# Gate tiles first in the input projection, with the start of the recurrence between its later tiles

## What is computed

```python
h = modulate(rmsnorm(x, ln1_w), shift, scale)
p = h @ w_in                 # 18 tiles of 128 columns
# au, av : 2+2 tiles, gating MLP          bq, bkv, kr : 2+1+1, latent attention
# cq, cf, cb, ci, cg : 2 each, recurrence (query, forget gates of both directions, value, output gate)
a = au * (w_s . rmsnorm(av) + b_s)
f, k = gates(cf, cb)         # log of the forget gate; key = 1 - gate
o = scan_forward(cq, k, ci, log f) + scan_backward(...)    # in chunks of 128 tokens
b = attention(...)
x += gate * (concat(a, b, rmsnorm(o) * silu(cg)) @ w_out)
x += gate * peer(modulate(rmsnorm(x), ...))                # expert retrieval; the longest part
```

## Time and profile before

| | us |
|---|---|
| median of 3 runs (lowest, highest) | 4656.94 (4653.06, 4658.84) |
| profiled execution, its own time | 4664.94 |
| its span, first to last instruction | 4662.7 |
| PE, DVE, ACT, POOL busy | 4049.6, 3641.3, 1752.6, 1137.1 |

### The profile page before, as it was taken

How to read it: one execution, slowest core, us unless ns; L and a number is a source line. 1 busy time by engine, 2 the same in 40 slices (tenths; PEclk the granted TensorE clock), 3 DMA queues, 4 the chain that set the end, 5 groups by cost and what they waited for, 6 DMA issues and landing times. The chain is left out here.

```text
span 4662.7 us, 66977 instructions
## 1 busy us (share of the span) xinstructions
PE 4049.6 (87%) x22357; PEld 3490.8 (75%) x22357; DVE 3641.3 (78%) x7170; ACT 1752.6 (38%) x3120; POOL 1137.1 (24%) x1190
## 2 busy tenths in 40 slices
PE   7967877899789999999999976788864899999998
PEld 6865435799678888888888855633653799999998
DVE  4177665699979999999999943734599799999998
ACT  3223542210334444444444432254312444444443
POOL 0000000000964343434434400000005632333332
PEclk9956999895999999999999978599987999999999
DMA  4110112124579999999999920000212799999997
GB/s 171 50 37 27 50 54 87 40 69 136 164 260 373 376 377 368 366 371 383 373 374 376 369 67 32 18 0 0 76 52 72 272 372 373 371 371 371 375 374 282
DMA packets 246327, 1017.96 MB, mean 218 GB/s; under 512 B 16976, under 2 KB 115376, under 8 KB 145984
## 3 DMA queue, kind: packets, MB, share of 16 engines
q0 software_dynamic: 85824, 602.70, 33.4%
q1 hardware_dynamic: 160320, 413.17, 24.5%
HBM read 963.31 MB, written 52.43 MB: 218 GB/s over the span
## 5 line engine op out<-in xcount | busy, mean ns | idle before, releaser
L479 PE MATMUL psA<-h_hi,split_hi 128*128 128x448 f32 (+3 forms) x2816 | 991.7, 352 | 128.0 <-DVE xT L2247 54.9
L1206 POOL DMA_INDIRECT rows<-rows,pick_i x512 | 795.8, 1554 | 1160.6 <-DVE y_tok L2268 651.3
L1704 DVE TENSOR_TENSOR split_lo<-raw,split_hi 128x1024 fp32r<-128x1024 f32 x596 | 727.1, 1220 | 417.0 <-ACT split_hi L1247 415.4
L479 PE MATMUL psA<-h_lo,split_hi 128*128 128x448 f32 (+3 forms) x2816 | 969.6, 344 | 0.0
L479 PE MATMUL psA<-h_hi,split_lo 128*128 128x448 f32 (+3 forms) x2816 | 969.2, 344 | 0.0
L1247 ACT ACTIVATE split_hi<-raw 128x1024 fp32r<-128x1024 f32 x596 | 628.1, 1054 | 317.4 <-DMA raw<-expert_pairs 147.2
L479 PEld LDWEIGHTS psA<-h_hi,split_hi 128*128 128x128 f32 x2816 | 535.7, 190 | 216.7 <-issue 140.9
L2256 DVE CUSTOM_DVE_ANT_1 rows<-rows,h_wide 128x1024 f32<-128x1024 f32 x512 | 624.0, 1219 | 16.5 <-DMA rows<-rows,pick_i 14.2
L2268 DVE SCALAR_TENSOR_TENSOR y_tok<-rows,pick_w,y_tok 128x1024 f32<-128x1024 f32 x444 | 568.6, 1281 | 5.9
L479 PEld LDWEIGHTS psA<-h_hi,split_lo 128*128 128x128 f32 x2816 | 536.1, 190 | 38.0
L479 PEld LDWEIGHTS psA<-h_lo,split_hi 128*128 128x128 f32 x2816 | 537.2, 191 | 34.3
(11 more groups left out here) (301 smaller groups left out, 6470.4 us busy)
## 6 DMA issues: line engine op xcount, KB each, us to landing
raw<-expert_pairs SPq DMA_DIRECT2D x256, 1024.0 KB, 7.2
gates<-g_buf SPq DMA_DIRECT2D x24, 2048.0 KB, 8.7
raw<-tiles SPq DMA_DIRECT2D x84, 512.0 KB, 3.5
raw<-mod_tiles SPq DMA_DIRECT2D x80, 512.0 KB, 3.4
g_in<-gates POOLq DMA_DIRECT2D x32, 896.0 KB, 8.8
g_in<-gates POOLq DMA_DIRECT2D x32, 640.0 KB, 5.8
mod_w<-mod_pairs SPq DMA_DIRECT2D x8, 1024.0 KB, 17.8
rows<-rows,pick_i POOLq DMA_INDIRECT x512, 8.5
```

What stands on the lines that cost most here:

```text
L479: ins = nc.tensor.matmul(out_, lhsT, rhs, start=start, stop=stop)
L1206: nc.gpsimd.indirect_dma_start(rows[l][:, b, :], None, (rows0, rows1)[l], bass.IndirectOffsetOnAxis(pick_i[:, u:u + 1], 0))\
L1704: V.tensor_tensor(split_lo[:, n % SPLIT].rearrange("p k n -> p (k n)"), raw[:, n % RAW, :], split_hi[:, n % SPLIT].rearrange("p k n -> p ( ...
```

## The change

The columns of `w_in` are put in the order cf, cb, av, cq, ci, kr, bkv, bq, cg, au. Steps of the chain whose inputs are then ready are moved between the later tiles: at step 3 the clip and the logarithm, at 4 the sums, at 5 the squares' sum, the root and the exponential, at 6 the norm of av, at 7 the multiplication by the key. Splits go one tile further ahead (`split_to(IN0 + p + 4)`). Results of tiles 14 to 17 (cg in `psV`, au in `psA`) stay in PSUM until the last tile is done, since their places in SBUF lie where the projection's input is. After them PE first transposes, then does the gating product. The first two `log_decays` stand before it on DVE. `MOD_FRONT` is gone: its 8 tiles are now worked off in `route`. POOL's clearing of `states` waits for the end of the projection in place of the end of the gating part.

```diff
-MOD_FRONT, MOD_OWN = 8, 32
+MOD_OWN = 32
-MOD_AFTER = (20, 7, 7, 6)
+MOD_AFTER = (26, 8, 8, 6)
+HELD_AT = 14
-    in_cols = np.concatenate([a_u, b_q, b_kv, kr_tile, c_q, c_f, c_b, c_g, a_v, c_i])
+    in_cols = np.concatenate([c_f, c_b, a_v, c_q, c_i, kr_tile, b_kv, b_q, c_g, a_u])
...
# PE
+                elif HELD_AT <= p < HELD_AT + 2:
+                    held[l].append(seen.bank(psum_V_free))
+                    feature_tile("V", own)
...
-                for i in range(MOD_FRONT):
-                    mod_tile(psA[:, f + 1, 2 * i:2 * i + 2], (OUT0[l] + i) % RAW)
             pe.wait_ge(khat_ready, seen.upto(khat_ready))
...
+            gated_mlp(l)
             pe.wait_ge(khT_ready, seen.upto(khT_ready))
...
# POOL
-            pool.wait_ge(a_done, seen.upto(a_done))
+            pool.wait_ge(proj_ready, seen.upto(proj_ready))
             pool.memset(states[:], 0.0).then_inc(states_zero, 1)
...
# ACT
+            for p in range(IN_TILES):
+                split_to(min(IN0[l] + p + 4, OUT0[l]))
...
+                if p == 5:
+                    value_root()
+                    e_powers()
+                if p in (5, 9) or p >= HELD_AT:
                     continue
...
+                if p == 3:
+                    act.sem_inc(gate_raw, 1)
+                    act.wait_ge(f_ready, seen.upto(f_ready))
+                    A(lf[:], lf[:], ACT.Ln).then_inc(logf_ready, 1)
...
+            for t in range(2):
+                copy_pair(banks[t], own, ACT.Copy, au[:, t]).then_inc(psum_A_free, 2)
...
+                    ins = A(cg[:, t, s:s + n], psV[:, f + b, 0:n], ACT.Silu)
...
# DVE
+            for p in range(IN_TILES):
+                split_to(min(IN0[l] + p + 4, OUT0[l]))
+                if p == 3:
+                    log_forget(l)
+                elif p == 4:
+                    decay_sums()
+                elif p == 5:
+                    value_squares(l)
+                elif p == 6:
+                    value_norm(l)
+                elif p == 7:
+                    decayed_keys()
...
+            dve.wait_ge(proj_ready, seen.upto(proj_ready))
+            log_decays(0)
+            log_decays(1)
+            gated_mlp(l)
```

More of the change, by code:

```diff
@@ L462, in build_program @@
     block = sem_ctx.enter_context(nc.Block())
-    front_bank = []
+    held = [[] for _ in range(DEPTH)]
     out_full = [[] for _ in range(DEPTH)]
@@ L579, in in_projection @@
             own, both = segs_of(l, False), segs_of(l, True)
[L580 to L584, removed]
+            for p in range(IN_TILES):
+                if p in (4, 8):
+                    token_pair(own if p == 4 else both)
+                elif HELD_AT <= p < HELD_AT + 2:
+                    held[l].append(seen.bank(psum_V_free))
+                    feature_tile("V", own)
+                    held[l].append(seen.n[psum_V_free])
+                elif p not in (5, 9):
+                    feature_tile("A", both if p < 4 or p in (10, 11) else own)
         def gated_mlp(l):
@@ L1301, in in_projection @@
             both = segs_of(l, True)
[L1302 to L1306, removed]
+            for p in range(IN_TILES):
+                split_to(min(IN0[l] + p + 4, OUT0[l]))
+                if p in (4, 8):
+                    token_values(av if p == 4 else ci, own if p == 4 else both)
+                    if p == 4:
+                        t0 = own[-1][0] // P
+                        A(av_sq[:, t0:], av[:, t0:], ACT.Square).then_inc(av_squared, 1)
+                        act.wait_ge(av_squared, seen.upto(av_squared))
+                    continue
+                if p == 5:
+                    value_root()
+                    e_powers()
+                if p in (5, 9) or p >= HELD_AT:
                     continue
@@ new lines, in in_projection @@
+            banks = []
+            for t in range(2):
+                banks.append(seen.bank(psum_A_full))
+                act.wait_ge(psum_A_full, seen.upto(psum_A_full, 2))
+            for t in range(2):
+                copy_pair(banks[t], own, ACT.Copy, au[:, t]).then_inc(psum_A_free, 2)
+                act.wait_ge(psum_A_free, seen.upto(psum_A_free, 2))
+            for t in range(2):
+                f, full = held[l][2 * t:2 * t + 2]
+                act.wait_ge(psum_V_full, full)
+                for b, (s, n, _) in enumerate(own):
+                    ins = A(cg[:, t, s:s + n], psV[:, f + b, 0:n], ACT.Silu)
+                ins.then_inc(psum_V_free, 2)
+                act.wait_ge(psum_V_free, full + 4)
@@ L1338, in gated_mlp, with e_powers @@
             act.wait_ge(a_root, seen.upto(a_root))
[L1340 to L1344, removed]
+        def e_powers():
             act.wait_ge(e_raw, seen.upto(e_raw))
@@ L1354, in hgrn @@
             act.sem_inc(khT_ready, 1)
-            A(lf[:], cb[:], ACT.Exp).then_inc(gx_exp, 1)
+            for d, part in enumerate((cb_f, cb_b)):
+                ins = A(lf[:, 2 * d:2 * d + 2], part[:], ACT.Exp)
+            ins.then_inc(gx_exp, 1)
             act.wait_ge(gx_exp, seen.upto(gx_exp))
@@ L2388, in _ @@
             norm(l, 0)
-            for t in range(IN_TILES):
-                split_to(min(IN0[l] + t + 3, OUT0[l]))
-            dve.wait_ge(proj_ready, seen.upto(proj_ready))
-            gated_mlp(l)
+            in_projection(l)
             hgrn(l)
```

210 lines of the change are left out of this document (96 added, 114 removed).

## The result

| | before | after |
|---|---|---|
| median of 4 runs (lowest, highest), us | 4656.53 (4653.06, 4658.84) | 4584.60 (4581.50, 4597.26) |
| span of the profiled execution, us | 4662.7 | 4579.3 |

The ratio is 0.9843, with an interval of 0.9831 to 0.9855: the changed kernel is 72 us faster, where 69 were forecast. The first thing to do with two such traces is to cut both at the same events and to compare piece by piece. I used the first DVE product on the norm's input, the end of the recurrence's units (the first load of `bc`), the load of `keysT` behind the attention and PE's first `onehot` product behind `route`. Layer 1 starts at ACT's first square of its norm; `bc` and `keysT` cut it as they cut layer 0.

What follows compares the result with a forecast made beforehand. Bound by a hand-over chain between engines after the projection, and by PE in the projection ahead of it. Terms -42.4 - 46.2 - 5.3 + 8.2 + 16.4 = -69.3 us take the median 4656.9 to 4588, range 4572 to 4606.

Steps and rivals of the forecast that it cites:

- Term 1: Layer 0, PE's last projection product to first `decayed`: chain falls from 79.9 to 37.5 us, gain 42.4.
- Term 2: Layer 1, same chain after the last projection tile: falls from 78.9 to 32.7 us, gain 46.2.
- Term 3: Projection: layer 0's old PE hole goes, gain 5.3 us; moved steps delay splits in layer 1, loss 8.2.
- the new hole: Layer 1's projection: PE stands 12 us awaiting tile 9's split, plus 1.9 us for the lowered clock.
- Term 4: `route`: eight more modulation tiles on PE take 26.4 us, less 10.0 of waiting used up: loss 16.4.
- the 10.0 of waiting: `route` before the change: PE stands 10.0 us before transposes; added tiles were to fill this first.
- Term 5: POOL's clearing beside `log_decays`: taken as 0, with 2.5 us a layer as the other bound.
- A: `route` hides the added modulation tiles, for instance through a higher clock: 4572 us; chance 6%.
- B: Layer 1's projection gets no new PE hole, so 12 and 1.9 us go: 4574 us; chance 7%.
- C: Projection: hole longer in layer 1 or also in layer 0, from dearer table loads: 4595 to 4605 us; 12%.
- D: Projection: PE's clock stays at 0.50 after the hole; about 4740 us if both layers suffer; 2%.
- E: Tile order makes PE wait elsewhere as long as before: 4650 to 4660 us; chance 2%.

Runs made afterwards that it cites:

- experiment 3: Changed kernel with clip, logarithm, decay sums, exponential and key product put back behind the projection's last tile: 4632.2 us.
- experiment 5: Changed kernel with DVE's two `log_decays` put back behind the states: 4598.9 us.
- experiment 1: Kernel before, with only the 8 early modulation tiles moved into `route`: 4682.1 us, ratio 1.0045.
- experiment 6: Changed kernel with PE's gating product placed ahead of the token tiles' transposes: 4579.6 us.
- experiment 4: The changed kernel itself run again, unedited, as reference on another chip: 4589.6 us.
- Experiment 2: Changed kernel with tiles 8 and 9 split ahead of the decay sums and roots: 4574.5 us.
- Experiment 10: Changed kernel with tiles 8 and 9 split first, gating product before transposes, and 16 modulation tiles on DVE in layer 0's attention: 4576.9 us.

## Why the prediction was right, term by term

The main claim was that the time after the last tile is a chain, not an engine's load, and that most of it could be worked off between tiles at no cost in layer 0. Experiments 3 and 5 put two parts of it back, and the time came back in the stages named: 25 and 6 of the 44.2 us in layer 0, 30 and 6 of the 46.5 in layer 1. That the other 13 and 10 us belong to the early norm of av, the held tiles and the changed order on PE follows by subtraction; they were not put back one by one. Experiments 1 and 6 took the 8 modulation tiles out and the gating product to the front, and moved the stage of layer 0 by under 1 us each.

- **Term 1**, -42.4: measured 79.9 to 35.7, so -44.2. The gating product was mis-sized, 5.39 for 3.24, since the clock stood at another level there. One step of the sum does not add up as written: four transposed tiles at 0.9 us behind 5.0 give 8.6 and not 9.3. The last one ended at 9.6, so that step came out near by luck.
- **Term 2**, -46.2: 78.9 to 32.4, so -46.5. The same slip is in it (3.9 and 3.6 give 7.5, not 8.1; measured 8.7), and the gating product took 2.78 us for 3.6.
- **Term 3**, -5.3 and +8.2: from the stage's start to PE's last projection product layer 0 took 172.3 us before and 167.3 after, so -5.0; layer 1 took 162.9 and 170.9, so +8.0 (+6.6 in experiment 4). Experiment 2 shows the new hole by its removal. The step that did not exist, the table load in the chain up to the logarithm, put 1.3 us too much into the 12; the other steps took 0.4 more than their rows.
- **Term 4**, +16.4: +16.9, and +17.0 in experiment 1. That the 10.0 of waiting is used up first was the right rule: eight tiles take 26.6 us and 16.9 arrive. Experiment 10 found the other side of it.
- **Term 5**, 0: as taken. And the clip's own 2.5 us, which lay inside term 1, goes with POOL's clearing wherever it was looked for: beside it 4.23 and 4.24 us, away from it 1.76 (both layers of the changed kernel, layer 1 of the kernel before and of experiment 3), and the scaling that met it in experiment 3 lost 2.4 us as well. The Trainium skill (SBUF — State Buffer, "Who interferes with whom") has both halves, the `tensor_scalar` that is held up and the two-input operation that a memset does not touch, and these rows agree.

Of the rivals, A and B ended away from the measured stages: `route` grew by 16.9 us, and the hole was 11.4 us long. C rested on a table load's costing more than its row; the load at 228.57 follows the drain before it and is followed at once by the next, so nothing was added. D's clock came back after 4 us. E would have left the time at 4650 to 4660.

Not foreseen were two shifts: the attention of layer 0 (-2.8), of which the last section says more, and the experts' stage (-9.9), where the profiled executions of kernels with the same experts lie between 1521 and 1536 us. So the forecast stands on its stages, which came out at -70.9 for -69.3; that the medians, at -72, agree as closely is partly luck, since a single execution scatters by more. The windows of the experts' stage show PE's clock at 0.99 and DMA at 0.91 to 0.92, in a short one (the changed kernel's, 1522.6 us) and a longer one (experiment 4's, 1531.0) alike. What differs is how long DVE waits for the `rows` that DMA gathers for the experts (from the view of waits: total, times, longest). The changed kernel:

```profile
DVE rows L2296 <- DMA rows<-rows,pick_i: 3.7, 7, 1.3
```

And experiment 4:

```profile
DVE rows L2296 <- DMA rows<-rows,pick_i: 10.7, 11, 1.6
```

Over all thirteen profiled executions this wait is 3.2 to 7.1 us where the stage takes up to 1526.2 us, 8.5 to 11.1 where it takes 1527.3 to 1531.0, and 13.1 to 14.2 above. That is a correlation; why the gathers land later in one execution than in another stays open. It is not the change, since two executions of the same changed kernel differ by it.

## What to carry to other kernels

When several engines idle at once, write down the chain that they hand over and ask which of its inputs is ready long before the chain starts; then order the work that makes the inputs so, and put the steps between other work. Every moved step stands ahead of something on its engine: follow the latest thing that must pass it (here the split of tile 9) against the work that the waiting engine still has, since that difference is the hole. And work that one stage hides costs its price in the next: count how much idle time the new place has, and stop there (8 tiles of DVE work in the attention paid, the next 8 did not).

## What the runs showed of the hardware

PE's granted clock can differ between two kernels in a stretch that neither edit touches, with PE just as busy. The same 9 us of layer 0's attention, 54 us after its start, first in the windows of the kernel before:

```profile
474.80:483.80 9.00, 6.83 (x19) 3.06 (x18) 7.54 (x8) 0.86 (x2) 0.00 (x0) 0.50 0.00 0
```

And in those of the changed kernel:

```profile
424.20:433.20 9.00, 6.83 (x26) 3.28 (x25) 7.57 (x8) 2.45 (x4) 0.00 (x0) 1.00 0.00 0
```

PE's busy time is the same; the clock is 0.50 in one and 1.00 in the other, and 19 products are done instead of 26. In the 18 us ahead of it PE is busy for 14.14 us in both, at 0.99 and 1.00; the first differences lie nearer the stage's start, where in its first 9 us PE is busy for 5.94 us in one and 6.38 in the other. Experiments 1 and 3, whose attention took 336.8 and 336.5 us, are with the kernel before (experiment 3 shows 0.50 there too); experiments 2, 4, 5 and 6, with 334.1 to 334.5, are with the changed one. A given kernel gives nearly the same stage in both executions that were profiled (333.8 and 334.2). In layer 1's attention the same thing is worth up to 4.6 us. What decides, an earlier pause or the finer order of the products, was not tried. So a gain or loss of 2 to 5 us in an unchanged stage is no sign that an edit works as meant, and in a comparison of versions the granted clock of the unchanged stages should be looked at before the medians are believed.
